# Hybrid decoder layer with a mixture of experts on one core: the last four experts' down matrices loaded and multiplied by column halves

## What is computed

```python
def add_expert(acc, params):
    wg, wu, wd, g = params
    hid = jax.nn.silu(t @ wg) * (t @ wu)
    return acc + g[:, None] * (hid @ wd).astype(jnp.float32), None

routed, _ = lax.scan(add_expert, jnp.zeros((n_tok, d), jnp.float32),
                     (w_gate_e, w_up_e, w_down_e, gates.T))
```

## Time and profile before

| | us |
|---|---|
| median of three runs | 585.91 (585.03 to 586.32) |
| the profiled execution | 586.18 |
| its span in the trace | 584.6 |
| TensorE busy | 554.6 (95%) |
| VectorE busy | 209.1 (36%) |
| ScalarE busy | 159.4 (27%) |
| loaded from HBM | 225.9 MB, 388 GB/s over the span |

### The profile page before, as it was taken

One profiled execution on the slowest core, in us unless ns is written; L12 is line 12 of the kernel. 1 busy time (PEld: TensorE's weight loads), 2 busy tenths in 40 slices (PEclk: granted clock), 3 DMA queues, 4 the chain that ended last, 5 costly groups with the idle time before them and its releaser, 6 DMA issues.

```text
span 584.6 us, 8347 instructions
## 1 busy us (share of the span) xinstructions
PE 554.6 (95%) x3168; PEld 308.6 (53%) x3169; DVE 209.1 (36%) x533; ACT 159.4 (27%) x308; POOL 24.3 (4%) x78
## 2 busy tenths in 40 slices
PE   8999999999999999999999989999999899779975
PEld 6988875465544444555455444544544444235322
DVE  2879788664335322220222221111222222121112
ACT  5787366342212222220222221122111122121102
POOL 1006230000000000000000000000000000000000
PEclk9999999999999999999999999999999999898989
DMA  8997559659999999999999999999999999999994
GB/s 315 419 419 297 210 198 424 270 198 373 415 424 418 422 420 420 426 427 425 428 424 423 427 421 432 421 425 432 421 426 427 428 423 429 423 424 422 422 408 163
DMA packets 27496, 227.50 MB, mean 389 GB/s; under 512 B 3264, under 2 KB 3392, under 8 KB 7744
## 3 DMA queue, kind: packets, MB, share of 16 engines
q1 hardware_dynamic: 27168, 226.67, 93.4%
q10 hardware_dynamic: 288, 0.29, 0.1%
HBM read 225.90 MB, written 1.05 MB: 388 GB/s over the span
## 4 chain that ended last, share of the span: by engine, by line
PE 72%; DMA 18%; SPq 4%; DVE 4%; issue 1%; ACT 1%; DVEq 0%; ACTq 0%
PE ps L1776 27%; PE ps L1805 11%; DMA cell_two<-in_w_e 9%; PE ps L1734 7%; PE ps L1834 5%; PE ps L1641 5%; DMA cell_gu<-in_w_e 5%; PE ps L1537 4%; SPq L473 4%; DMA cell_three<-in_w_e 3%; PE ps L1504 3%; PE ps L1518 2%; PE ps L1796 1%; PE ps L1526 1%; DMA wA<-in_w_qk 1%
## 5 line engine op out<-in xcount | busy, mean ns | idle before, releaser
L1776 PE MATMUL ps<-cell_two,xg 128*64 128x512 f32 (+2 forms) x576 | 115.9, 610 | 13.1 <-DMA cell_two<-in_w_e 11.2
L1805 PE MATMUL ps<-cell_d,e_hT 128*64 128x512 f32 (+2 forms) x464 | 89.8, 597 | 2.1 <-DVE e_hT L1396 2.1
L1776 PEld LDWEIGHTS ps<-cell_two,xg 128*64 128x64 f32 (+2 forms) x576 | 37.3, 130 | 89.4 <-issue 89.3
L1776 PE MATMUL ps<-cell_gu,xg 128*64 128x512 f32 (+2 forms) x416 | 80.3, 613 | 1.9 <-DMA cell_gu<-in_w_e 1.8
L1393 DVE TENSOR_TENSOR e_h<-e_sg,ps 128x256 f32<-128x256 f32 x28 | 11.8, 422 | 183.4 <-ACT e_sg L911 183.4
L911 ACT ACTIVATE e_sg<-ps 128x256 f32<-128x256 f32 x28 | 10.8, 385 | 205.1 <-PE ps L1776 205.1
L1461 DVE SCALAR_TENSOR_TENSOR ylo<-ps,gslot,yhi 128x512 fp32r<-128x512 f32 (+1 forms) x53 | 39.1, 740 | 72.5 <-ACT yhi L922 72.5
L1734 PE MATMUL ps<-pick,xhi 128*128 128x256 f32 x224 | 58.5, 300 | 0.3 <-DVE pick L1309 0.3
L922 ACT ACTIVATE yhi<-ps,gslot 128x512 fp32r<-128x512 f32 (+1 forms) x53 | 35.9, 679 | 70.0 <-PE ps L1805 70.0
L1734 PE MATMUL ps<-pick,xlo 128*128 128x256 f32 x224 | 54.4, 281 | 0.0
L1776 PEld LDWEIGHTS ps<-cell_gu,xg 128*64 128x64 f32 (+2 forms) x416 | 26.3, 131 | 50.9 <-issue 50.7
(11 more groups left out here) (342 smaller groups left out, 675.2 us busy)
## 6 DMA issues: line engine op xcount, KB each, us to landing
cell_two<-in_w_e SPq DMA_DIRECT2D x36, 2048.0 KB, 26.7
cell_d<-in_w_e SPq DMA_DIRECT2D x56, 1024.0 KB, 25.9
cell_gu<-in_w_e SPq DMA_DIRECT2D x48, 1024.0 KB, 18.4
cell_three<-in_w_e SPq DMA_DIRECT2D x4, 3072.0 KB, 21.5
wo<-in_w_out SPq DMA_DIRECT2D x1, 4096.0 KB, 12.4
wA<-in_w_qk SPq DMA_DIRECT2D x7, 512.0 KB, 11.2
wR<-in_w_rest SPq DMA_DIRECT2D x3, 1024.0 KB, 28.5
wV<-in_w_v SPq DMA_DIRECT2D x1, 2048.0 KB, 18.9
```

The source lines that it names most:

```text
L1776: last = mm(ps[side * w:(side + 1) * w, U, :], rows(k, slice(side * w, (side + 1) * w)), weight[:, k - k0, :], start=k == 0, stop=k == KD - 1)
L1805: last = mm(ps[side * w:(side + 1) * w, Y[half], :], e_hT[:, kk, side * w:(side + 1) * w], n[:, kk, half * 512:(half + 1) * 512], start=kk ...
```

## The change

1. The loop at L585 loads for each of the last four experts the left 512 columns of both input halves; the loop at L591 loads the right 512 columns of both, expert by expert, each under a semaphore of its own. Both are 512 KB in runs of 2 KB, so eight issues stand where twelve stood.
2. TensorE runs the whole left half of the down matmuls, then for each expert, when its right half has landed, both quarters with both `kk` (`down_quarters`). The scatter of the left half stands between the second and the third expert.
3. ScalarE and VectorE copy the left half of the result before they evacuate the quarters.
4. In the last group's high part, two matmuls of `keep_clock` stand after the wait for the second expert's matrix, and two after the third's.
5. The router bias shares the router weights' semaphore, and TensorE waits for both; the unused semaphore of `wA[0]` is gone.

```diff
-            sp.dma_start(rbias[:], router_bias[0].partition_broadcast(P)).then_inc(rb_loaded, 16)
+            sp.dma_start(rbias[:], router_bias[0].partition_broadcast(P)).then_inc(rt_loaded, 16)
...
-                    sp.dma_start(cell_d[i][:, 0:1], ranked("down", chosen[e - first])[:, 0:1]).then_inc(cell_loaded[i], 16)
+                    c = slice(0, 512)
+                    sp.dma_start(cell_d[i][:, :, c], ranked("down", chosen[e - first])[:, :, c]).then_inc(cell_loaded[i], 16)
...
-            for half in range(2):
-                c = slice(half * 512, (half + 1) * 512)
-                for e in groups[-1].experts:
-                    sp.dma_start(cell_d[cell_of["down", e]][:, 1:KH, c],
-                                 ranked("down", chosen[e - first])[:, 1:KH, c]).then_inc(tail_loaded[half], 16)
+            c = slice(512, D)
+            for n, e in enumerate(groups[-1].experts):
+                sp.dma_start(cell_d[cell_of["down", e]][:, :, c], ranked("down", chosen[e - first])[:, :, c]).then_inc(tail_loaded[n], 16)
...
                     nc.scalar.mul(yhi[:, c], o, gslot[:, g.routed % 2:g.routed % 2 + 1]).then_inc(yhi_act, 1)
+                    if g is groups[-1] and i == 0:
+                        act.wait_ge(residual_ps, 1)
+                        result(0, 1)
...
+                    if g is groups[-1] and i == 0:
+                        dve.wait_ge(residual_ps, 1)
+                        result(0, 2)
...
-            pe.wait_ge(rt_loaded, 16)
+            pe.wait_ge(rt_loaded, 32)
...
+            def down_quarters(cells, side):
+
+                w = P // len(cells)
+                for c, o in results_of(groups[-1])[1:]:
+                    for kk in range(KH):
+                        last = mm(o[side * w:(side + 1) * w, :], e_hT[:, kk, side * w:(side + 1) * w], cells[side][:, kk, c],
+                                  start=kk == 0, stop=kk == KH - 1, skip_group_check=True)
+                    if side == len(cells) - 1:
+                        last.then_inc(y_ps, 1)
...
                         wait_loaded(pe, part, e)
+                        if part == "high" and g is groups[-1] and e in g.experts[1:3]:
+                            keep_clock(2)
...
-                    down(cells, y_ps, (0,), range(KH - 1))
-                    for kk in range(KH - 1):
-                        for quarter in range(2):
-                            down_quarter(cells, kk, quarter)
-                    pe.wait_ge(tail_loaded[0], 16 * g.n)
-                    down(cells, y_ps, (0,), range(KH - 1, KH))
-                    pe.wait_ge(tail_loaded[1], 16 * g.n)
-                    for quarter in range(2):
-                        down_quarter(cells, KH - 1, quarter)
+                    down(cells, y_ps, (0,))
+                    for side in range(g.n):
+                        if side == 2:
+                            pe.wait_ge(S_act, NR)
+                            pe.wait_ge(yhi_act, 2 * (NR - 1) + 1)
+                            pe.wait_ge(ylo_dve, 2 * (NR - 1) + 1)
+                            scatter(S, last_ps, halves=(0,))
+                        pe.wait_ge(tail_loaded[side], 16)
+                        down_quarters(cells, side)
```

More of the change, by code:

```diff
@@ L330, in hybrid_decoder_layer @@
             memT_loaded, x_loaded, mem_loaded, vec_loaded, wg_loaded, wV_loaded, kv_loaded, wo_loaded, x1_loaded,
-            rt_loaded, rb_loaded, consts, zeroed, ssq_act, std_act, xn_dve, diag_dve, row_ps, row_act,
+            rt_loaded, consts, zeroed, ssq_act, std_act, xn_dve, diag_dve, row_ps, row_act,
             xT_act, xT_dve, unit_ps, unit_act, unit_dve, conv_dve, z_ps,
@@ L342, in hybrid_decoder_layer @@
         ) = [ctx.enter_context(nc.semaphore(name)) for name in """
-            memT_loaded x_loaded mem_loaded vec_loaded wg_loaded wV_loaded kv_loaded wo_loaded x1_loaded             rt_loaded rb_loaded consts zeroed ssq_act std_act xn_dve diag_dve row_ps row_act xT_act xT_dve
+            memT_loaded x_loaded mem_loaded vec_loaded wg_loaded wV_loaded kv_loaded wo_loaded x1_loaded             rt_loaded consts zeroed ssq_act std_act xn_dve diag_dve row_ps row_act xT_act xT_dve
             unit_ps unit_act unit_dve conv_dve z_ps bc_act mask_pool w_dve
@@ L354, in hybrid_decoder_layer @@
         wA0_half = [ctx.enter_context(nc.semaphore(f"wA0_half{i}")) for i in range(2)]
-        wA_loaded = [ctx.enter_context(nc.semaphore(f"wA_loaded{n}")) for n in range(8)]
+        wA_loaded = {n: ctx.enter_context(nc.semaphore(f"wA_loaded{n}")) for n in range(1, 8)}
         wR_loaded = [ctx.enter_context(nc.semaphore(f"wR_loaded{g}")) for g in range(3)]
-        tail_loaded = [ctx.enter_context(nc.semaphore(f"tail_loaded{i}")) for i in range(2)]
+        tail_loaded = [ctx.enter_context(nc.semaphore(f"tail_loaded{i}")) for i in range(groups[-1].n)]
         cell_loaded = [ctx.enter_context(nc.semaphore(f"cell_loaded{i}")) for i in range(CELLS + 1)]
@@ L951, in _ @@
             group(groups[-1])
-            act.wait_ge(residual_ps, 1)
-            for half in range(2):
-                result(half, 2 * half + 1)
+            result(1, 3)
             act.wait_ge(out_act, 2)
@@ L1281, in _ @@
             evac_x2T(1, 0)
-            dve.wait_ge(rb_loaded, 16)
+            dve.wait_ge(rt_loaded, 32)
             dve.wait_ge(consts, 3)
@@ L1479, in _ @@
             group(groups[-1])
-            dve.wait_ge(residual_ps, 1)
-            for half in range(2):
-                result(half, 2 * half + 2)
+            result(1, 4)
         @block.tensor
@@ L1995, in _ @@
             group(groups[-1])
[L1996 to L1999, removed]
             for quarter in range(2):
```

## The result

| | median, us | runs, us |
|---|---|---|
| kernel before | 585.83 | 10, from 585.03 to 587.88 |
| kernel after | 588.26 | 10, from 587.43 to 589.92 |

The ratio is 1.0042, with a 95% interval of [1.0029, 1.0054]. I had forecast 586.3, no change that can be told, with a range of 584.8 to 588.6. The time lies in the range, but on the slower side, 2.0 us above the forecast. The range was wide enough to take in several rivals; the case that I held likeliest was wrong, and a rival came true. The profiled execution of after took 588.15, of which 586.4 are its span.

What follows compares the result with a forecast made beforehand. Weight loads bound the kernel until the last landing at 576.7, then TensorE's tail. Span 584.6 + 0.47 (last copy) - 0.3 (output) = 584.8, the clock's 1.7 spent on right passes; 584.75 + 1.58 = 586.3, range 584.8 to 588.6.

Steps and rivals of the forecast that it cites:

- (b): Right-half down matmuls: TensorE reaches the second expert only after four passes of the first; 587.7 us, chance 0.11.
- (c): Last high half or narrow passes from 574 on: the clock still falls, 1.7 less 0.15 hidden; 587.9 us, chance 0.08.
- (d): Loads: the last right half lands late by up to 1.5, with 0.4 hidden; 587.8 us at most, chance 0.02.
- I take overlap: Right-half down matmuls: two neighbouring experts' passes share the array, a pair costing 1.72, four experts 3.44 against 1.72 before.
- the 0.28 behind the landing: First right-half pair: of the 0.86 added by shallow overlap, 0.28 is hidden by the second expert's landing.
- (a): Right-half down matmuls: strict program order, no pass starts before those ahead, a pair takes 3.2; 589.0 us, chance 0.12.
- the 0 that I took for their delay: Before the last high half: four spare matmuls fill TensorE's hole and delay the real start by 0 to 0.1, taken as 0.
- The fall of the clock: Last high half: spare matmuls prevent the drop to 1.2 GHz, saving 1.7; worth only 0.7 in the kernel before.
- Loading by halves: Last down-matrix loads: eight issues replace twelve for the same 4 MB; bounds -0.3 to +1.5, taken as 0.
- Output: End of the kernel: with half the bytes out earlier, the last output takes 2.3 instead of 2.6, -0.3.
- The copies of the left half: ScalarE and VectorE tail: left copies, 0.6 and 0.7, finish by 578.0 before the first right quarter, so free, 0.3 to spare.
- The +0.4 against the median: Whole kernel: the kernel after should differ by +0.4 from the median of before, whose runs mix executions with and without the fall.

Runs made afterwards that it cites:

- the last version: Kernel after with right halves loaded as eight 256 KB row pieces, four experts always alternating around the left scatter, two more spare matmuls: 585.57, ratio 1.0001 to before.

## Why the prediction was wrong

The time fell within the range because the range took in rivals (b), (c) and (d); the mechanism that I summed up was not the one that ran.

- **The step that failed: "I take overlap: a pair costs 1.72, and the four experts 3.44 against 1.72 before."** A pair costs twelve slots, 2.58, and its drain, not eight. It is rival (b), 587.7, to which I gave 0.11: "if the second expert is reached only after four passes of the first, each pair takes 0.86 more". Against the forecast the first pair came out 0.58 later (0.86 less the 0.28 behind the landing) and the second 0.86. The rows that I relied on the earlier trace rows have four passes on each tile, and of the numbers measured four is the largest that costs nothing. I had noted the difference (eight here) and drew on them all the same: beyond what they show, they could not speak.
- **Rival (a), strict order, is out.** In the kernel after the second expert's first pass begins after four of the first one's, not after eight. The Trainium skill's rule ("TensorE: Matmul & The Clock Gate", Part 3: matmuls in program order, only weight loads pulled ahead) doesn't hold for narrow tiles here: its order gives a pair 15 slots, 3.2 us, where the trace has twelve, 2.58. Where the experts change every four passes, it would give 13 slots, 3.0 with the drain (my estimate from the same 0.215), where the trace has 1.93.
- **The sum otherwise.** The last high matrix landed 0.4 later, at 566.87, and TensorE started the high half at 566.88, 0.30 later than in before. The spare matmuls ended at the same moment, 566.84: they took 1.97 where I had put 1.72 without the drain, and began at 564.87 and not 564.6. So this profile doesn't tell which of the two held TensorE; with four experts in turn it was the spare matmuls (564.31 to 566.28, the high half at 566.22 without a wait), so the 0 that I took for their delay is not safe. From 566.88 on every link up to down kept its length (down at 572.59, forecast 572.27). 0.32 + 0.58 + 0.86 = 1.76; the left scatter was as long as forecast. The quarters' evacuation began 0.02 after the pair's end and not 0.12, which gives 0.1 back. The last copy ended at 583.56 (forecast 581.88), the span 2.84 later (forecast 2.9). With 0.17 more outside the span (below) that makes 586.33 + 1.8 = 588.15. One slip beside the sum: rival (d) with 0.4 of its 1.5 hidden comes to 587.4, not 587.8.
- **The fall of the clock** went as forecast in the profile (3.64, clock 1.00), and my reading that it was worth 0.7 and not 1.7 holds: 7.9 against 7.1 behind the last landing. But it was there in one profile of three, and neither in before nor in after did the spare matmuls move the median by anything that can be told. The forecast set its 1.7 of gain against 1.7 of cost; the gain is there only in an execution with a fall.
- **Loads, outputs, tail.** Loading by halves: zero, as taken, though four of its issues stood over 4 us on SyncE. Output: the last landed in 2.4, forecast 2.3. The copies of the left half lay ahead of the quarters (577.84 to 579.01; ScalarE's quarter began at 580.13), free.
- **Rival (c), the clock in the narrow passes,** is refuted for this profile: the granted clock (the third column from the right) is 1.00 from 575 to 580 although in the pairs only one or two tiles work.

```profile
575.00:580.00 5.00, 5.00 (x31) 2.67 (x30) 1.44 (x2) 0.91 (x2) 0.00 (x0) 1.00 0.20 77
```

- **The +0.4 against the median.** The kernel with alternating pairs is the one that my sum described: 586.48, and 1.1 above the kernel before on its chip. So even had the pairs overlapped, the change would have cost 0.2%, not 0.07%. I set 586.33, worked out from an execution with the fall taken away, against a median of three runs of 585.91; the two profiled executions without a fall took 585.20 and 585.26.

## What to carry to other kernels

When narrow float32 matmuls share TensorE's array, let the neighbours alternate every one or two matmuls in program order: here an order that finished one tile's eight passes before the next gave up half of the sharing, with the landings waited for beforehand or not. A trace row that shows an overlap proves it for the run length that the row has; the first thing to count is how many passes in a row stand on one tile. And before a stall is priced, take a second and third profile: what the first execution showed was in one of three here, and the wait for the last landing hid more than half of its cost.

## What the runs showed of the hardware

- **Look-ahead of TensorE between column tiles**, in passes of 256 columns of float32: eight passes on one tile ahead of another cost the other four slots (2.81), six cost two (2.35, 2.38), four and two cost none (1.93, 1.92). Which count inside TensorE sets this is open.
- **The granted clock fell behind idle time, not in narrow work.** It stayed at 2.4 GHz through the pairs on one or two tiles (575 to 580 in after). With four experts in turn it fell to 1.2 GHz at 577.0, after a hole of 1.80, and with that hole filled it did not. A hole of 1.81 before the high half was followed by a fall; holes of 1.38, 1.23 and 0.78 in the same place were not, nor was one of 1.77 elsewhere.
- **Outside the span** lie 1.56 to 1.60 us in the five profiles that end like the kernel before (it, twice more, spare matmuls alone, the last version) and 1.70 to 1.80 in the eight others. I did not find out why; 0.17 of the loss is this.
